# A conditioning row turned by four transposes and summed by VectorE, in a two-block transformer kernel on one NeuronCore

## The reference, cut to what matters

```python
s_lat = jax.nn.silu(c)
s_ctx = jax.nn.silu(c_ctx)
for i in range(DEPTH):
    sh1, sc1, gt1, sh2, sc2, gt2 = jnp.split((s_lat @ ada_w[i] + ada_b[i])[:, None, :], 6, axis=-1)
    sh1c, sc1c, gt1c, sh2c, sc2c, gt2c = jnp.split(s_ctx @ ada_w[i] + ada_b[i], 6, axis=-1)
    h = x * (1.0 + sc1) + sh1
    hc = ctx * (1.0 + sc1c) + sh1c
    ...
```

## Time and profile before

| what | us |
|---|---|
| median of three executions | 4185.95 |
| span of the profiled execution | 4179.4 |
| TensorE busy | 3880.4 (93%) |
| VectorE busy | 2160.6 (52%) |
| ScalarE busy | 1670.0 (40%) |
| GpSimd busy | 617.0 (15%) |

### The profile page before, as it was taken

The page is one execution under the profiler, slowest core; times in us unless marked ns, Lnnn a source line. Parts: engine busy times, 40 slices in busy tenths (PEclk is TensorE's granted clock), DMA queues, the critical chain, the costliest instruction groups (busy, mean ns, idle before and its releaser), DMA issues.

```text
span 4179.4 us, 67654 instructions
## 1 busy us (share of the span) xinstructions
PE 3880.4 (93%) x28266; PEld 3183.4 (76%) x28266; DVE 2160.6 (52%) x3078; ACT 1670.0 (40%) x2711; POOL 617.0 (15%) x676
## 2 busy tenths in 40 slices
PE   6999999789999989987999899999999998899999
PEld 4877777668888867756788675778888877778887
DVE  3667754753222453377324654555665428655564
ACT  4445455422112341264223336544334435544333
POOL 0045555421000001003000000000210003000120
PEclk9999999888999999999999899999999999999999
DMA  5243454321211121103232320222223230312332
GB/s 162 79 144 125 157 163 153 108 88 61 71 61 61 58 81 61 41 1 112 84 98 91 66 81 11 83 91 72 97 95 108 81 111 4 133 62 82 101 101 81
DMA packets 235991, 367.67 MB, mean 88 GB/s; under 512 B 9811, under 2 KB 142630, under 8 KB 235302
## 3 DMA queue, kind: packets, MB, share of 16 engines
q1 hardware_dynamic: 217200, 300.49, 21.8%
q0 software_dynamic: 17936, 62.70, 4.9%
q10 hardware_dynamic: 550, 0.17, 0.0%
HBM read 344.36 MB, written 18.96 MB: 87 GB/s over the span
## 4 chain that ended last, share of the span: by engine, by line
PE 75%; DVE 15%; ACT 7%; issue 2%; DMA 1%; ACTq 0%; POOL 0%; DVEq 0%; SPq 0%; POOLq 0%
PE psum L259 21%; PE psum L261 20%; PE psum L260 20%; PE psum L256 12%; DVE arena L289 4%; ACT arena L389 3%; PE psum L265 2%; DVE arena L299 2%; DVE rw L289 2%; DVE rx L383 2%; DVE arena L303 1%; ACT rw L393 1%; DVE arena L295 1%; DVE arena L315 1%; ACT rx L393 1%
## 5 line engine op out<-in xcount | busy, mean ns | idle before, releaser
L259 PE MATMUL psum<-rx,rw 128*128 128x512 f32 (+2 forms) x2864 | 1057.8, 369 | 47.0 <-DVE rx L383 28.2
L260 PE MATMUL psum<-rx,rw 128*128 128x512 f32 (+2 forms) x2864 | 1030.5, 360 | 0.0
L261 PE MATMUL psum<-rx,rw 128*128 128x512 f32 (+2 forms) x2864 | 1028.6, 359 | 0.0
L289 DVE TENSOR_TENSOR rw<-arena,rw 128x2048 fp32r<-128x2048 f32 (+3 forms) x266 | 549.8, 2067 | 811.5 <-ACT rw L393 802.1
L256 PE MATMUL psum<-arena 32*32 32x32 f32 (+10 forms) x12982 | 762.8, 247 | 112.8 <-ACT arena L393 41.2
L256 PEld LDWEIGHTS psum<-arena 32*32 32x32 f32 (+5 forms) x12982 | 580.6, 133 | 256.1 <-issue 84.8
L393 ACT ACTIVATE rw<-arena 128x2048 fp32r<-128x2048 f32 (+3 forms) x266 | 453.6, 1705 | 753.4 <-PE psum L261 737.6
L259 PE MATMUL psum<-rw,rx 128*128 128x512 f32 (+1 forms) x1720 | 680.9, 396 | 31.1 <-DVE rx L383 13.8
L259 PEld LDWEIGHTS psum<-rx,rw 128*128 128x128 f32 (+1 forms) x2864 | 550.6, 192 | 181.8 <-DVE rx L383 40.6
L260 PE MATMUL psum<-rw,rx 128*128 128x512 f32 (+1 forms) x1720 | 672.5, 391 | 0.0
L261 PE MATMUL psum<-rw,rx 128*128 128x512 f32 (+1 forms) x1720 | 672.3, 391 | 0.0
(11 more groups left out here) (73 smaller groups left out, 2216.6 us busy)
## 6 DMA issues: line engine op xcount, KB each, us to landing
arena<-in_ffn_w_up SPq DMA_DIRECT2D x66, 1024.0 KB, 5.0
arena<-in_ada_w SPq DMA_DIRECT2D x48, 1024.0 KB, 6.6
arena<-in_ffn_w_down SPq DMA_DIRECT2D x40, 1024.0 KB, 4.9
arena<-in_ffn_w_gate SPq DMA_DIRECT2D x22, 1024.0 KB, 5.1
arena<-in_dn_w_in SPq DMA_DIRECT2D x16, 1024.0 KB, 6.0
arena<-in_xa_w_kv SPq DMA_DIRECT2D x16, 1024.0 KB, 5.0
arena<-in_hgrn_w_in SPq DMA_DIRECT2D x16, 1024.0 KB, 5.4
arena<-in_da_w_in SPq DMA_DIRECT2D x12, 1024.0 KB, 5.0
```

Source lines behind the costliest of these rows:

```text
L259: self.e.matmul(out, l[0], r[0], start=start, stop=False)
L260: self.e.matmul(out, l[0], r[1], start=False, stop=False)
L261: return self.e.matmul(out, l[1], r[0], start=False, stop=stop)
L289: return self.e.tensor_tensor(out, a, b, op)
```

## The change

In `pe_ada_turn` the four products with the selection matrix become four transposes. Each writes a 128 x 128 block, so that the bank is filled: column 128m+32k+r holds partial sum k of vector r for block m. In `dve_ada_mod` VectorE reads the columns with r of 0 and 1, adds the four partial sums in one reduction into 8 columns of scratch (`tmpc`, columns 128 to 135), and then adds these to `modT`. The bank is set free behind the reduction. The signal `mod` comes from the second instruction. The 24 pieces all go this way.

```diff
@@ -609,7 +609,7 @@ def pe_ada_turn
     p.wait_ge(*K.at("ada_row", i, pc))
     b = p.bank("ada_T", i, pc, among=among)
     for m in range(4):
-        ins = p.mm(b[:, 2 * m:2 * m + 2], ada_row(K)[:, m * 128:(m + 1) * 128], K.mem(CO + 832, 2))
+        ins = p.tr(b[:, m * 128:(m + 1) * 128], ada_row(K)[:, m * 128:(m + 1) * 128])
     ins.then_inc(*p.sig(("ada_T", i, pc)))
     p.close("ada_T", i, pc)
 
@@ -658,8 +658,11 @@ def dve_ada_mod
     v.wait_ge(*K.at("ada_T", i, pc))
     md = K.modT[i][:, pc * 4:pc * 4 + 4, :]
-    v.tt(md, md, K.ps("ada_T", i, pc)[:, 0:8].rearrange("p (m r) -> p m r", r=2), ADD).then_inc(*v.sig(("mod", i, pc)))
+    part = K.tmpc[:, 128:136].rearrange("p (m r) -> p m r", r=2)
+    got = K.ps("ada_T", i, pc)[:, :].rearrange("p (m k r) -> p m r k", m=4, r=32)[:, :, 0:2, :]
+    v.red(part, got, ADD).then_inc(*v.sig())
     v.free("ada_T", i, pc)
+    v.tt(md, md, part, ADD).then_inc(*v.sig(("mod", i, pc)))
```

## The result

The changed kernel takes 4197.01 us (median of 6 runs, 4193.15 to 4200.17) where the kernel before, run beside it on the same chip, takes 4185.9 us (6 runs, 4181.1 to 4188.02). The ratio is 1.0029, with a 95% interval of 1.0018 to 1.0041. The forecast was 4179.8 us, at most 4190.0.

The account below looks back on a forecast made before the run. The chain ran through TensorE for 75% of the span and VectorE for 15%. TensorE's -8.0 and VectorE's +1.8 made -6.2 us, from 4185.95 to about 4179.8 us, called no change; range 4174.7 to 4190.0.

Parts of the forecast that it names:

- TensorE's 8.0 us: Turns on the chain: transposes save 2 x 0.87 early, 0.87 at one half-clock side turn, 15 x 0.36 at others.
- the rival in which they save nothing: At the turns: transposes issued as two passes, TensorE's term about nothing, +1.8 us remain, 4187.8 us; chance 0.06.
- VectorE's durations: Each piece: reduction 190 ns, gap 100, addition 167 replace an addition of 164; 0.29 us more, 1.8 on six chain additions.
- The early part: First four turns, within 53 us: two on the chain save 0.87 us each; two before the context's load save nothing.
- At the other 18 pieces I cost it at nothing: Pieces whose addition is off the chain: VectorE's extra 0.29 us each was priced at zero.
- the cover is VectorE's own idle time: Side pieces: VectorE's idle time hides its extra; if gone everywhere, 14 others cost 14 x 0.29 = 4.1 us more.
- VectorE pays at all side pieces: Units between 300 and 520 us and beyond: 20 x 0.29 less 1.7, +4.1 us, 4190.0; chance 0.14.
- VectorE pays nowhere: All side turns: TensorE's saving counts at every one, VectorE's addition costs nothing; -9.4 us, 4176.5; chance 0.14.
- The clock falls: Side turns near waits: transposes lower TensorE's clock, 1.75 us per low stretch; at ten turns +11.3 us, 4197.3; chance 0.06.
- The signs: Wrong if, among others, side-turn distance does not shrink some 4.5 us, VectorE waits grow over 2, or half-clock stretches over two.
- the sum of -6.2 us: Whole kernel: TensorE's saving of 8.0 us less 1.8 for six VectorE additions on the chain; chance 0.60.

Follow-up runs that it names:

- e2: Kernel before with four transposes and VectorE's one addition, of the first partial sum only (other three left out); 4188.65 us against 4182.67, ratio 1.0010.
- e6: Kernel before with transposes, first partial sum only added, and GpSimd's state multiplication waiting for VectorE's subtraction; 4149.8 us, ratio 0.9929 to the kernel before.
- e4: Kernel before with one wait added: GpSimd's state multiplication waits for VectorE's subtraction of the same unit; 4158.84 us, ratio 0.9940 to the kernel before.
- e11: Repeat of e4 (kernel before, GpSimd's state multiplication waits for VectorE's subtraction); 4154.75 us, ratio 0.9932 to the kernel before.
- e1: Kernel before, products kept, with VectorE taking their columns through an added reduction before the addition; 4186.73 us against 4182.67, ratio 1.0011.
- e3: Changed kernel with one wait added: GpSimd's state multiplication waits for VectorE's subtraction of the same unit; 4157.53 us, ratio 0.9941 to the kernel before.
- e10: Repeat of e3 (changed kernel, GpSimd's state multiplication waits for VectorE's subtraction); 4157.3 us, ratio 0.9934 to the kernel before.
- e5: Kernel before, products kept, with VectorE's added reduction and GpSimd's state multiplication waiting for VectorE's subtraction; 4158.8 us, ratio 0.9948 to the kernel before.
- e9: Changed kernel with side pieces' addition one round later and GpSimd's state multiplication waiting for VectorE's subtraction; 4148.55 us, ratio 0.9917 to the kernel before.
- e8: Changed kernel with the side pieces' addition to modT one round later, no wait added; 4186.62 us against the kernel before's 4183.46, ratio 1.0013.
- e7: Kernel before with the opposite wait: VectorE's subtraction waits for GpSimd's state multiplication of the same unit; 4231.66 us against 4180.31, ratio 1.0126.

## Why the prediction was wrong

**TensorE's 8.0 us.** The transposes go in one pass each, and the rival in which they save nothing falls. But 0.36 us for a side turn at full clock was too little, and so was the upper bound of 0.40. What counts for TensorE is the time from the turn's start to the start of its next instruction, and that fell from 0.81 to 0.36 us, by 0.45. Before and then changed, one turn and what follows it:

```profile
323.92 0.95 PE L256 MATMUL psum<-arena 128*128 128x2 f32 x8
324.74 0.36 PE L259 MATMUL psum<-rx,rw 128*128 128x256 f32 x1
...
326.24 0.60 PE L265 MATMUL psum<-arena 128*128 128x128 f32 x4
326.59 0.36 PE L259 MATMUL psum<-rx,rw 128*128 128x256 f32 x1
```

In e2, which has as much time at half clock among the side turns as before, TensorE is busy 9.9 us less there (488.97 against 498.89):

```profile
227.00:754.30 527.30, 488.97 (x9102) 403.19 (x9101) 356.89 (x639) 265.46 (x578) 280.82 (x374) 0.95 0.48 153
```

So the forecast did not fail on this term; it was too small. With the order fixed, e6 lies 9.0 us under e4 and 5.0 under e11; they ran beside different runs of the kernel before, and by the ratios, each good to some 5 us, it is 4.6 and 1.3. So a gain of this size fits the times, and they do not settle it to a few us.

**VectorE's durations.** 192 and, but for one addition (below), 167 ns against 190 and 167. The gap between the two was over-estimated: 0.10 us was forecast, and at 327.67 + 0.19 to 327.90 it is 0.04, so a piece costs VectorE 0.23 us more, not 0.29.

**The early part.** The transposes of the early turns at half clock were to bring 1.7 us. From the landing of the context's load (32.62, changed 36.09) to the start of ScalarE's work on the second part (53.81, changed 54.80), before took 21.2 us and the changed kernel 18.7, 2.5 us less. All of it lies behind the start of the third turn (46.37, changed 49.83). That turn, at half clock in both, takes 1.05 us to the next instruction in place of 1.80, a saving of 0.75 where 0.87 was forecast. From the fourth turn's start to ScalarE it is 1.27 us in place of 3.00, because that stretch was granted 1.00 in this execution and 0.50 in the one before. So the 2.5 us mix the saving with a clock that was higher in this execution; twice 0.75 us, an estimate from the third turn, would be 1.5 of the 1.7 forecast. The load itself landed 3.5 us later, after a load of `ada_b` that took 5.12 us in place of 2.73.

**The step that failed** is "At the other 18 pieces I cost it at nothing", with the reason given for the side pieces, that "the cover is VectorE's own idle time". I asked whether 0.29 us fits into VectorE's idle time as a sum (76% busy between 300 and 520 us). It does not have to fit into a sum but into the lead at one place: behind `kS`, where the idle time was 0.14 to 0.22 us and GpSimd's multiplication stood 0.22 us behind the subtraction. Of that idle time 0.10 us is the gap that VectorE leaves between two such instructions anyway, so the lead to lose was 0.26 to 0.34 us. By e1 the change takes 0.23 us off it on VectorE's side, which is not quite enough, and by e2 some 0.45 on TensorE's (the saving of one turn), since a faster TensorE releases GpSimd earlier. Of GpSimd I wrote only that no instruction is added to it, and I took the durations of all unchanged instructions as fixed. What the runs showed in place of that nothing: the same 96 copies took 9.7 us longer, TensorE's waits for VectorE grew by 12.6 us, and with the order fixed by a wait both kernels became some 24 us faster than the kernel before and the difference between them went. The profile of before held the sign. The wait of 1.78 us at 526.95 that I used stands behind four copies of 3.61 us, in VectorE's timeline of before:

```profile
522.89 3.61 DVE L315 COPY arena<-arena 32x128 f32<-32x128 f32 x4
```

where the unit at 329.58 needs 1.17 for the same four. I read the wait as VectorE being busy and did not ask with what.

An estimate: four more slow units at 3.4 us make 13.6 us; with the two parts netting nothing in e3, e4, e10 and e11, that fits the 11 us measured, within its interval (7.5 to 17 us).

**The rivals.** *VectorE pays at all side pieces* had the right engine and the wrong mechanism: its 4.1 us came from 20 times 0.29, where few pieces pay and those pay over 3 us each, and e2 shows that TensorE's saving turns them without VectorE. In part it may hold beside that: e5 leaves room for some us of VectorE's own time. *VectorE pays nowhere* falls. *The clock falls* came near in time (4197.3), and the signs that I named for it did show: 64.9 us at half clock in the side part against 51.2. But e2 has the transposes and 51.2, and e3 has them and 23.9. The mean granted clock of whole executions, over all runs of a kernel, says the same: with the order fixed it is 0.970 without transposes in the turns (e4, e11) and 0.970 with them (e6, e9; for e3 and e10 see below). Without that wait it is 0.966 in the 21 runs of before that stood beside e1 to e4, 0.964 in e2, e8 and the changed kernel, and 0.963 in e7, which has the old products and the longest waits. The rule of the Trainium skill ("TensorE: Matmul & The Clock Gate", Part 4: PE-mode transpose) would have had e6 and e9 lose clock, and they do not. The first transposes behind the context's load are a second row against it. In the changed kernel the first 14 took 0.21 us each and the last 10 took 0.11, and the pace doubled at 39.10, while TensorE had done nothing but transpose since 36.09:

```profile
36.09 3.18 PE L265 MATMUL psum<-arena 128*128 128x128 f32 x14 [3.91 <-DMA arena<-in_ctx]
...
39.10 1.26 PE L265 MATMUL psum<-arena 128*128 128x128 f32 x10
```

The same happens in the kernel before at 37.4 us, after 22 of the 24.

**The signs.** The distance of the side turns was to shrink by 4.5 us and grew by 10; the waits for VectorE were to grow by no more than 2 and grew by 12.6; the stretches at half clock were to grow by no more than two and went from 9 to 12. All three were named as signs of being wrong, and the waits pointed at the right place.

**With the order fixed**, the sum of -6.2 us still does not appear (-1.3 and +2.6), while e9, which moves only the small addition by one round, lies 8.8 us under e10. It is not that VectorE's additions stand on the path at more pieces: in e3's chain that ended last they stand at five of the 20 side pieces, fewer than the six before. What differs on record is the mean granted clock of whole executions: 0.9684 over the runs of e3 and again of e10, 0.9698 to 0.9704 in e4, e11, e5, e6 and e9. An estimate from these: some 12 us more at half clock in an execution, worth up to 6 us. Why the clock is lower with both parts in one round is not shown.

**Open.** The 10.3 us of the side stretch can be split. TensorE stands idle 13.0 us more in it (539.80 - 496.17 against 529.50 - 498.89), of which 12.7 are waits for VectorE. It is busy 2.7 us less, and that is an estimated 9 us from 20 turns at 0.45, less what 13.7 us more at half clock cost, up to 6.9 us. At which waits the clock falls stays open: from the last run of TensorE ahead of the unit near 329 us to its next stage the changed kernel lost 2.5 us (328.11 to 338.33 against 326.25 to 333.95) at a clock of 1.00, and a stretch at 0.50 follows the unit near 474 us. The pause of 0.46 us near 474 us has no known cause either, and it is not known why the clock rose earlier among the 24 early transposes in one execution than in the other.

## What to carry to other kernels

An instruction's duration is not its own where two engines work on SBUF at once: before costing an edit at nothing, look for pairs of VectorE and GpSimd instructions that are released by the same event, and at the lead between them. A lead of some 0.3 us that no semaphore holds can be lost by any edit, also by one that makes another engine faster. A shape whose mean is far above its shortest (453 ns against some 270 here) shows such a pair, and one wait that fixes the order can be worth more than the edit under study: 24 us here, against 6 forecast.

## What the runs showed of the hardware

- VectorE and GpSimd on SBUF: the 128x512 subtraction took 0.69 us when first and 1.1 to 1.6 us with GpSimd's 128x512 multiplication begun 0.01 to 0.48 us ahead, the less the longer ago it began; the multiplication took 1.03 us when first and 1.37 when 0.22 us behind.
- Four 32x128 copies took 1.06 us in sum when they were done before or just after GpSimd's 128x640 multiplication began, and 3.47 when they began just after it: 1.43, 0.50, 0.22 and 1.32 us, the first, second and fourth each ending 0.08 to 0.10 us behind an instruction of GpSimd.
- Even the 8-column addition can be caught: at 443.18 of the changed kernel it took 0.93 us in place of 0.17, beside a GpSimd multiplication that ran from 443.05 for 1.03 us. That is why its group's mean is 191 ns above and not 167.
- A reduction of 32 PSUM elements a partition into 8 took 192 ns; the line through the sizes of the earlier trace rows (1.05 ns an element) held down to it.
- Four 128x128 fp32 transposes held TensorE for 0.36 us to its next instruction at full clock, the eight passes of four two-column fp32 products for 0.81.
- A wait added on GpSimd cost nothing that shows, and the mean granted clock of the side part rose from 0.95 before to 0.97 in e4.
